# Three expert buffer sets in turn for the first experts, the block count moved behind the first expert, and a first pair without zero scatters

## What is computed

```python
g_prob = softmax(hf @ w_group + b_group)           # 8 groups
g_w, g_idx = top_k(g_prob, 1)
e_logits = (hf @ w_expert + b_expert).reshape(T, 8, 8)
e_sel = e_logits[arange(T), g_idx[:, 0]]
top_v, top_i = top_k(e_sel, 2)                     # 2 experts of the chosen group
gate = g_w * softmax(top_v)
...                                                # tokens sorted by expert into blocks
def expert_block(xb, e):                           # w1, w3: [64, 1024, 512], w2: [64, 512, 1024]
    return (silu(xb @ w1[e]) * (xb @ w3[e])) @ w2[e]
...
out = zeros(T + 1, D).at[row_token].add(row_gate[:, None] * ys)
```

## Time and profile before

| | us |
|---|---|
| median of 3 runs (lowest, highest) | 2045.76 (2043.47, 2046.9) |
| the profiled execution, device time | 2041.24 |
| the profiled execution, span | 2039.4 |
| PE busy in the span | 1771.7 |
| mean rate of the DMA engines over the span | 248 GB/s |

### The profile page before, as it was taken

One profiled execution on the slowest core, in us unless ns is written; L12 is line 12 of the kernel. 1 busy time (PEld: TensorE's weight loads), 2 busy tenths in 40 slices (PEclk: granted clock), 3 DMA queues, 4 the chain that ended last, 5 costly groups with the idle time before them and its releaser, 6 DMA issues.

```text
span 2039.4 us, 37905 instructions
## 1 busy us (share of the span) xinstructions
PE 1771.7 (87%) x15198; PEld 1252.6 (61%) x15198; DVE 917.9 (45%) x1756; ACT 723.6 (35%) x1325; POOL 265.0 (13%) x281
## 2 busy tenths in 40 slices
PE   7999999887877777787778777779989999999998
PEld 5677778644434443343434334358867799998877
DVE  5455335433322322232232223366275698886245
ACT  4444422432222222222222222153365554444143
POOL 0000000000000000000000000640010068880000
PEclk9999999999988988898898889889999999999999
DMA  6222233789999999999999999944230233333222
GB/s 209 78 84 66 73 103 144 273 335 420 427 424 427 425 426 426 425 426 425 426 425 426 425 426 426 423 146 123 79 91 5 73 99 118 106 104 121 96 83 83
DMA packets 109218, 505.66 MB, mean 248 GB/s; under 512 B 9640, under 2 KB 59176, under 8 KB 75984
## 3 DMA queue, kind: packets, MB, share of 16 engines
q1 hardware_dynamic: 101024, 492.07, 60.8%
q10 hardware_dynamic: 6512, 8.42, 1.6%
q0 software_dynamic: 1600, 4.02, 0.8%
HBM read 496.80 MB, written 2.11 MB: 245 GB/s over the span
## 4 chain that ended last, share of the span: by engine, by line
PE 61%; DMA 28%; DVE 5%; ACT 2%; issue 2%; SPq 1%; ACTq 0%; DVEq 0%
DMA ring<-in_w 27%; PE bank L700 13%; PE bank L702 13%; PE bank L701 13%; PE bank L2660 9%; PE bank L2588 3%; PE bank L2651 3%; PE bank L890 2%; PE bank L916 1%; PE bank L902 1%; DVE w_split L807 1%; SPq L2150 1%; PE bank L2673 1%; DMA raw<-in_w_in 1%; PE bank L1238 1%
## 5 line engine op out<-in xcount | busy, mean ns | idle before, releaser
L2660 PE MATMUL bank<-ring,XTs 128*32 128x256 f32 x4032 | 290.8, 437 | 140.5 <-DMA ring<-in_w 139.6
L2931 DVE TENSOR_TENSOR x<-x,bank 128x512 f32<-128x512 f32 x264 | 163.8, 681 | 510.1 <-PE bank L2651 509.3
L2660 PEld LDWEIGHTS bank<-ring,XTs 128*32 128x32 f32 x4032 | 145.0, 123 | 288.7 <-issue 237.1
L2408 ACT ACTIVATE y<-bank 32x256 f32<-32x256 f32 x256 | 95.9, 375 | 223.6 <-PE bank L2651 136.8
L2673 PE MATMUL bank<-ring,aT 128*32 128x256 f32 x2016 | 121.8, 382 | 57.4 <-DVE aT L2956 57.4
L700 PE MATMUL bank<-hT_all,w_split 128*128 128x512 f32 x362 | 146.4, 405 | 8.3 <-DVE ks_raw L2793 3.0
L807 DVE TENSOR_TENSOR w_split<-raw,w_split 128x2048 fp32r<-128x2048 f32 (+4 forms) x47 | 98.2, 2095 | 121.2 <-ACT w_split L791 121.0
L702 PE MATMUL bank<-hT_all,w_split 128*128 128x512 f32 x362 | 142.7, 394 | 0.0
L701 PE MATMUL bank<-hT_all,w_split 128*128 128x512 f32 x362 | 142.4, 393 | 0.0
L2588 PE MATMUL bank<-arena,oh 128*32 128x256 f32 x2048 | 136.2, 409 | 3.9 <-issue 0.9
L2651 PE MATMUL bank<-y,g 64*128 64x512 f32 x528 | 131.4, 615 | 2.8 <-ACT y L2408 1.8
(11 more groups left out here) (473 smaller groups left out, 3683.6 us busy)
## 6 DMA issues: line engine op xcount, KB each, us to landing
ring<-in_w SPq DMA_DIRECT2D x189, 2048.0 KB, 19.9
raw<-in_w_in SPq DMA_DIRECT2D x25, 1024.0 KB, 5.6
late_raw<-in_w_gate SPq DMA_DIRECT2D x11, 1024.0 KB, 5.4
late_raw<-in_w_up SPq DMA_DIRECT2D x11, 1024.0 KB, 5.3
late_raw<-in_w_down SPq DMA_DIRECT2D x11, 1024.0 KB, 5.0
raw<-in_w_out SPq DMA_DIRECT2D x4, 1024.0 KB, 5.2
third<-in_w SPq DMA_DIRECT2D x2, 2048.0 KB, 9.1
raw<-in_w_o SPq DMA_DIRECT2D x4, 1024.0 KB, 5.6
```

What stands on the lines that cost most here:

```text
L2408: act.activation(y2[to:to + BLK, Q * (j % 2):Q * (j % 2 + 1)], Yb[BLK * j:BLK * (j + 1), :], ACT.Copy).then_inc(y_out, 1)
L2660: mm = pe.matmul(Hb[BLK * j:BLK * (j + 1), :], XTs[u][:, 4 * (c % 2) + 2 * h + c // 2, :], w[:, at_:at_ + Q], start=(h == 0 and c == 0), s ...
L2931: ins = v.tensor_tensor(xs, xs, Sb[t % 2][n][:, :], ALU.add)
```

## The change

1. ACT's six router transfers are issued by POOL, in the same place of the program (after the attention's last read), in another order.
2. The copy of the last turned piece goes from DVE to ACT, as `turned(3, 1)` between the rows of tiles 0 and 1 and the squares of tile 3.
3. `starts` and `further` on PE, and the DVE steps that end in `m_ready` (now `dve_blocks`), go into the first pair: PE multiplies both halves of expert 0's `hidden` first; `dve_blocks` stands behind the first block's `act_out`. On DVE `ready()` (the second block's one-hot matrix) comes ahead of the wait for `starts`. ACT, PE and SP read the count later: ACT after its first pair, PE and SP after three.
4. The first pair has no scatters and no flushes: the semaphores are stepped instead, and POOL's two memsets go.
5. The third set takes a regular part: expert e goes to set e % 3 for e up to 5 and again 6 and 7 to sets 0 and 1, each load waiting for the block three before. From expert 8 on the loops are as before, with two sets. SP waits for `w_used` of six experts before it loads `gain_fin`.

The core of the diff (the router's transfers on POOL, the moved parts of `dve_route`, and semaphore helpers shortened):

```diff
428.95 1.93 PE L2673 DVE, dve_route
             v.sem_inc(S("r_over"), 1)
             columns(1, 0)
+            ready()
             full(v, J["starts"][0])
...
             v.tensor_tensor(low, inside, rel, ALU.mult).then_inc(S("r_further"), 1)
-            ready()
+        def dve_blocks(v, chain):
...
428.95 1.93 PE L2673 SP
+            def load_third(m, expert):
+                if m < 2:
+                    load_matrix(0, m, expert, third[m], S("third"))
+                    return
+                src = weights[2][expert:expert + 1].rearrange("a (h p r) n -> p (a h) (r n)", h=2, p=P)
+                sp.dma_start(ninth[0][:, 0:4, :].rearrange("p k n -> p (k n)"), src[:, 0, :]).then_inc(S("ninth"), 16)
+                sp.dma_start(ninth[0][:, 4, :], src[:, 1, 0:512]).then_inc(S("ninth"), 16)
+                sp.dma_start(ninth[1][:, :, :].rearrange("p k n -> p (k n)"), src[:, 1, 512:2 * D]).then_inc(S("ninth"), 16)
...
-            sp.wait_ge(w_used, 2)
-            for m in range(2):
-                load_matrix(0, m, 4)
-            sp.wait_ge(w_used, 4)
-            load_matrix(0, 2, 4)
-            for m, done in enumerate((2, 2, 4)):
-                sp.wait_ge(w_used, STEPS + done)
-                load_matrix(1, m, 3)
-            for m, done in enumerate((2, 2, 4)):
-                sp.wait_ge(w_used, 3 * STEPS + done)
-                load_matrix(1, m, 5)
+            for e in range(3, 8):
+                for m, done in enumerate((2, 2, 4)):
+                    sp.wait_ge(w_used, STEPS * (e - 3) + done)
+                    if e % 3 == 2:
+                        load_third(m, e)
+                    else:
+                        load_matrix(e % 3, m, e)
+            sp.wait_ge(w_used, STEPS * 6)
...
-            with sp.Fori(2, count) as i:
+            with sp.Fori(3, count) as i:
428.95 1.93 PE L2673 ACT
             read(act, J["att_v"])
-            for lo, n, w in ((0, NG, a["w_group"][0]), (NG, NE, a["w_expert"][0])):
-                act.dma_start(w_r[:, :, lo:lo + n], cols_of(w, 0, n)).then_inc(S("w_r"), 16)
-            row(r_row[:, 0:NG], "b_group", NG, S("w_r"))
-            row(r_row[:, NG:NR], "b_expert", NE, S("w_r"))
-            act.dma_start(scratch[:, 0:128 + BLK * (EB + 1)], a["route_consts"]).then_inc(S("w_r"), 16)
-            act.dma_start(r_gain, a["params"][:, slice(*PARAM_COLS["ffn"])]).then_inc(S("w_r"), 16)
...
             rows_scaled(1)
+            full(act, J["router"][0])
+            turned(3, 1)
             squares(3)
...
-            act.wait_ge(m_ready, 1)
-            count = act.value_load(...)
-            row(pos2.bitcast(I32), "positions_2", T, S("w_pos2"))
...
-            with act.Fori(0, count) as i:
+            act_pair(0, False)
+            act.wait_ge(m_ready, 1)
+            count = act.value_load(...)
+            row(pos2.bitcast(I32), "positions_2", T, S("w_pos2"))
+            with act.Fori(1, count) as i:
428.95 1.93 PE L2673 PE, pe_pair
+                    k, n = buffers[u]
+                    place = third if k == 2 else ring[3 * k:3 * k + 2]
                     pe.wait_ge(xt_out, 2 * i + (u + 1))
+                    columns_there(k, n)
                     hidden(u, 0, place)
-                    if at_once and u == 0:
+                    if first and u == 0:
                         hidden(u, 1, place)
+                        starts()
                     if u == 0 or not last:
                         pe.wait_ge(made_oh, 2 * i + (u + 2))
                         gather(1 - u)
-                    if u == 0:
+                    if first and u == 0:
+                        further()
+                        pe.sem_inc(s_filled, 2)
+                    if u == 0 and not first:
                         pe.wait_ge(g_out, i + 1)
                         pe.wait_ge(y_out, 8 * i + 8)
                         scatter(i, 0)
                         scatter(i, 1)
...
-                    if u == 0:
+                    if first and u == 0:
+                        pe.sem_inc(s_filled, 2)
+                    elif u == 0:
                         scatter(i, 2)
                         scatter(i, 3)
-            pe_pair(0, False, at_once=True)
-            pe_pair(1, False, third)
+            pe_pair(0, False, ((0, 1), (1, 1)), first=True)
+            pe_pair(1, False, ((2, 1), (0, 2)))
+            pe_pair(2, False, ((1, 2), (2, 2)))
...
-            with pe.Fori(2, count) as i:
-                pe_pair(i, False)
-            pe_pair(count, True)
+            with pe.Fori(3, count) as i:
+                pe_pair(i, False, ((0, i), (1, i)))
+            pe_pair(count, True, ((0, count), (1, count)))
428.95 1.93 PE L2673 DVE
-            job = J["hT2"][2 * NT - 1]
-            full(v, job)
-            full(v, J["router"][0])
-            free(v.tensor_copy(xT[1][1], by_chunk(job)), job)
...
+                    if u == 0 and first:
+                        v.sem_inc(flushed, 2)
+                        dve_blocks(v, chain)
+                    elif u == 0:
                         flush(i, 2)
                         flush(i, 3)
428.95 1.93 PE L2673 POOL
+            read(pool, J["att_v"])
+            for lo, n, w in ((0, NG, a["w_group"][0]), (NG, NE, a["w_expert"][0])):
+                pool.dma_start(w_r[:, :, lo:lo + n], cols_of(w, 0, n)).then_inc(S("w_r"), 16)
...
             pool.wait_ge(S("h2"), NT)
-            chain(pool.memset(y2[:, :], 0.0))
-            chain(pool.memset(g2[:, :], 0.0))
```

More of the change, by code:

```diff
@@ L2662, in hidden, with down @@
                 mm.then_inc(w_used, 1)
[L2664 removed]
+            def down(u, h, k):
                 for r in range(2):
@@ L2677, in _, with columns_there, rows_there, pe_pair @@
             for job in J["before_moe"]:
[L2678 removed]
+                if job.bank not in (0, J["starts"][0].bank, J["further"][0].bank):
                     claim(pe, job)
[L2681 to L2684 removed]
+            def columns_there(k, n):
+                if k == 2:
+                    pe.wait_ge(S("third"), 32 * n)
+                else:
+                    pe.wait_ge(landed[3 * k], 16 * n)
+                    pe.wait_ge(landed[3 * k + 1], 16 * n)
+            def rows_there(k, n):
+                if k == 2:
+                    pe.wait_ge(S("ninth"), 48 * n)
+                else:
+                    pe.wait_ge(landed[3 * k + 2], 16 * n)
+            def pe_pair(i, last, buffers, first=False):
                 for u in range(2):
[L2686 removed]
+                    k, n = buffers[u]
+                    place = third if k == 2 else ring[3 * k:3 * k + 2]
                     pe.wait_ge(xt_out, 2 * i + (u + 1))
[L2688 to L2695 removed]
+                    columns_there(k, n)
                     hidden(u, 0, place)
[L2697 removed]
+                    if first and u == 0:
                         hidden(u, 1, place)
+                        starts()
                     if u == 0 or not last:
@@ L2707, in pe_pair @@
                         scatter(i, 1)
-                    if not (at_once and u == 0):
+                    if not first or u:
                         hidden(u, 1, place)
@@ L2712, in pe_pair @@
                         rows_to_columns()
+                    if first and u == 1:
+                        for job in J["before_moe"]:
+                            if job.bank in (J["starts"][0].bank, J["further"][0].bank):
+                                claim(pe, job)
                     if u == 1:
```

76 lines of the change are left out of this document (33 added, 43 removed).

## The result

The changed kernel takes **2029.2 us** (median of 4 runs, 2028.33 to 2031.05) against 2045.51 us (4 runs, 2043.47 to 2046.9): ratio 0.9922, 95% interval 0.9905 to 0.9939. That is 16.3 us less; the interval reaches from 12.5 to 19.4 us. In a second series (after_again, 5 runs against 29 of the kernel before) the ratio is 0.9936 [0.9923, 0.9949], or 13.1 us.

The account below looks back on a forecast made before the run. The prediction took the DMA weight stream, full at 425 GB/s, to bound the mixture and PE to bound the stretch before it. From 2045.76, -2.5 and -9.5 (together -12.0) gave 2033.8 us, range 2030 to 2038.5.

Parts of the forecast that it names:

- The rival that HBM's supply sets the limit: From 400 us on the stream is already near its ceiling, so only some 4 and 2.5 us return: 2039; chance 0.01.
- Part 1, -2.5 us: Before the mixture, router transfers issued by POOL make `w_split` ready earlier, so PE's idle time ahead of it goes: -2.5 us.
- the gap: PE's one standstill shortly before the mixture, 2.52 us of waiting for `w_split`, ending at 256.25 us.
- Part 5, -9.5 us: Nine buffers in turn close the breaks in the weight stream from 400 to 452 us: -9.5 us, bounds 8.9 to 11.8.
- The subtracted 0.92 us: Stream loss in the cut-up `ninth` transfers, 400 to 408 us, expected a second time for expert 5: 0.92 us.
- The sum: The whole gain, all after 250 us and before 462: -2.5 - 9.5 = -12.0 us.
- Parts 3 and 4 through `w_used`: Early first expert without zero scatters lets SP load again sooner: first `hidden` at 399.7, loads allowed by 405.0 us.
- The wait for the count: PE waits up to 3 us before the gather for expert 2; path cost nothing, cover 2 to about 5 us.
- Part 2: The copy on ACT delays the normed rows about 0.6 us: 0 on the path, 0.4 us on PE's first block.
- the 18.4 us of the earlier trace: Read as PE's first wait for weights in the mixture, beginning at 461.2 us and lasting 18.4 us.
- PE does not lag: Its rival: `w_used` comes over 2 to 5 us late, the store runs dry, 5 to 9 us gained, about 2039; chance 0.08.
- the third set does what it says: Its rival: with six or more transfers queued the rate falls, only -2.5 to -4 us, 2042.5; chance 0.04.

Follow-up runs that it names:

- after_again: The changed kernel without any further edit, timed again in more rounds; ratio 0.9936 to the kernel before.
- pool_only: The kernel before with only the six router transfers moved from ACT to POOL; ratio 0.9981 to the kernel before, 3.9 us faster.
- late_count_3: The changed kernel with 15 more tiny copies in `dve_blocks`, which make the block count late; ratio 0.9933 to the kernel before.
- late_count_12: The changed kernel with 60 more tiny copies in `dve_blocks`, which make the block count later still; ratio 0.9988 to the kernel before.

## Why the prediction was right or wrong, point by point

- **The direction, the place and the cause** were right. All that the edits gain lies between 239 and 462 us; the stream is full from 408 on. The rival that HBM's supply sets the limit is out: the 52 us from 400 to 452 now carry 21.5 MB (by the four windows: 2.9, 1.7, 13.5 and 3.3) where the earlier trace rows had 17.1. That is 413 GB/s as their mean. The Trainium skill (DMA: Bandwidth & Descriptors, Bandwidth) gives 358 GB/s as what one core gets with both cores of its HBM domain streaming, and measured 425 for one core with the other idle. The prediction left this condition out. One core runs here, and the trace agrees with the second figure.
- **Part 1, -2.5 us: the term that failed.** The prediction's step was "0 if something else holds the Sigmoids, 2.5 if nothing does; I take 2.5", with the gap as upper bound. It measured -3.9 us, timed (pool_only, 2.0 to 5.7), and 4.2 in the traces from the last `ofTl` to the last L702: 2.7 where the clock stays, 4.2 to 5.6 where it falls. The gap had a price behind it that the one profile at hand didn't show, a stretch at half clock, in 5 of 7 traces, which costs 1.6 us. So the upper bound of 2.5 was wrong, and the range had no room for it. With the timed term the sum is -13.4, and 2045.76 gives 2032.4.
- **The Trainium skill's rule beside it** (Trainium Kernel Development and Optimization, Key Constraints) is that another issuing engine saves only issue time. The trace agrees as far as ACT goes: what it was rid of are the 6.1 us of its six issues. But "the gain is the gap alone", which I had drawn from the rule, did not hold. No lock-out of POOL's descriptors was seen, six issues from 239.05 to 243.0; but DVE was busy for only 0.69 of these 4 us, so this was hardly put to the test.
- **Part 5, -9.5 us:** measured -10.6 in the mixture. The subtracted 0.92 us for the second cut-up `ninth` was wrong: its matrix flows between 446 and 454 us, and 444 to 452 stands at 417, lacking 0.15 us. The first one was right: 400 to 408 still stands at 364, lacking 1.15 us. So the cut-up load cost about 1 us where nothing was queued behind it, and almost nothing with others behind it; that this is the reason was not tested. It makes 0.8 of the 1.1 us. The rest lies within the bounds of 8.9 to 11.8 that I gave.
- **The sum** with both measured terms is -3.9 - 10.6 = -14.5 us, between the timed 16.3 [12.5, 19.4] of 4 runs and 13.1 [10.4, 15.7] of the second series. From 2045.76 that is 2031.3; in range. By the 13.1 us of the second series it would be 2032.7. So whether the time falls just outside the range or just inside is within the scatter of four runs, whose single values lie 2.7 us apart, and the last 2 us can't be given to a step. The wrong term of part 1 stays wrong either way.
- **Parts 3 and 4 through `w_used`** were right in the mechanism: first `hidden` at 398.78 (said: 399.7), loads allowed at 402.50 (405.0 at worst), `down` of expert 0 ends at 408.97 (413.8 at worst). PE was at full clock, 3.66 us for the 64 matmuls, where 5.29 was the worst case. What I hadn't said is that most of it is part 4's: without the third set the scatters alone bring 5.8 of the 6.5 us.
- **The wait for the count** came as said, 2.08 us before the gather for expert 2, and costs the path nothing. Its cover is about 3 us by late_count_3 and late_count_12 (said: 2 to 5).
- **Part 2** at nothing on the path: not run alone. The last `third` load is issued 9.6 us behind the last L702 (9.1 before), so its margin of about 1.9 us was used by 0.5.
- **The marks later on:** the two ring loads are issued at 383.55 (said: near 385), and DVE's first reader of the router's weights starts at 308.20 without a wait. The first long wait for weights is 6.89 us at 495.72, at expert 8's `hidden`, as said; expert 7's has 1.12. The end of the mixture is 13.8 us earlier (said: some 12).
- **A reading that was wrong:** the 18.4 us of the earlier trace rows are no wait of PE. They are a load's way from its issue to its landing, and PE works during most of them. What PE waits there, for expert 6's weights, is 3.79 us, in order of time:

```profile
479.73 3.06 PE L2660 MATMUL bank<-ring,XTs 128*32 128x256 f32 x32 [3.79 <-DMA ring<-in_w]
```

  That the weights bound the mixture stands on the 425 GB/s over 838 us all the same. And the full rate begins with the tenth slice and holds for seventeen, not sixteen.
- **The rivals:** PE does not lag; the third set does what it says; PE's clock is 1.00 from 400 to 462 in the changed kernel's profile; in after_again it falls once (0.78 in the window from 410 to 416) and the mixture is no longer for it.

## What to carry to other kernels

A gap in TensorE's work can cost more than its length when PE is the bound behind it: look at the granted clock right behind it, in more than one profile. When a stream that bounds the kernel has breaks, count them by their causes (nothing used yet, no buffer free): cures for different breaks added here, and leaving out work that filled only zeros closed most of the first (1.2 us lacking from 24 to 44, where the early product leaves 0.03 and the old code 2.9 to 4.5). And where a few us matter, compare stretches that begin and end at the same two instructions, as from the last `ofTl` to the last L702, where six traces agree to 0.02 us, and not whole spans or starts counted from zero.

## What the runs showed of the hardware

- A gap of 2.3 to 2.5 us in TensorE's work was followed by half clock in 5 of 7 executions and by full clock in 2 of 7, with the same code around it; the fall cost 1.6 us. At one place of the second block such falls come not at all, once or twice, with the same code, and the block takes 686.5 to 690.5 us.
- ACT took 3.59 us to issue one small load (`b_group`) behind two with many short pieces; POOL issued the same loads in 0.54 to 0.92 us each.
- Taking the first iteration of ACT's loop out ahead of it removed two table loads of 1.28 us in each of 28 iterations. Why was not tried.
- At a granted clock of 1.00 matmuls of one form started every 0.229 us up to about 333 us and every 0.233 us from there on; in two of 13 traces the second spacing began at about 260 us.
- One core's loads ran at 425 GB/s for 828 us, and at 417 to 423 from 408 us to 452.
